# A two-block transformer on one core: the mixer's heads without rotation or mean matmuls, their ends split, inverse roots on GpSimd

## The reference, cut to what matters

```python
p = h @ w_in                                    # split into rq rk rv rg gq gf gi gg ca cb gates
q = _rope(heads(rq, 4), positions)              # [t1*cos - t2*sin, t1*sin + t2*cos], halves of 64
k = _rope(heads(rk, 4), positions) * 128 ** -0.5
o = _retention(q, k, heads(rv, 4))              # o_t = sum_{s<=t} gamma^(t-s) (q_t.k_s) v_s
mu = o.mean(-1, keepdims=True)
o = (o - mu) * lax.rsqrt(jnp.square(o - mu).mean(-1, keepdims=True) + 1e-5)
u_a = o * ret_norm_g * jax.nn.silu(rg)

o = _hgrn2(silu(gq), logf, -expm1(logf), gi)    # gated recurrence, chunkwise
o = o * lax.rsqrt(jnp.square(o).mean(-1, keepdims=True) + 1e-5)
u_b = o * hgrn_norm_g * jax.nn.silu(gg)

u_c = silu(layer_norm(causal_dwconv(ca * sigmoid(cb), 31 taps)))
y  = sigmoid(gates0) * (u_a @ w_branch[0]) + sigmoid(gates1) * (u_b @ w_branch[1])
y += sigmoid(gates2) * (u_c @ w_branch[2])
return y @ w_out
```

## Time and profile before

| what | value |
|---|---|
| median of 3 runs | 3512.76 us (3499.04 to 3517.75) |
| the profiled execution's own time | 3506.1 us |
| its span, first to last instruction | 3504.3 us |
| mean granted TensorE clock | 0.986 of full speed |
| TensorE busy | 3335.8 us, 15280 matmuls |
| VectorE, ScalarE, GpSimd busy | 2126.9, 1306.1, 616.4 us |
| mixer of layer 0, from its first piece | about 1524 to 2110 us of the span |
| mixer of layer 1 | about 2514 to 3090 us of the span |

### The profile page before, as it was taken

How to read it: one execution, slowest core, us unless ns; L and a number is a source line. 1 busy time by engine, 2 the same in 40 slices (tenths; PEclk the granted TensorE clock), 3 DMA queues, 4 the chain that set the end, 5 groups by cost and what they waited for, 6 DMA issues and landing times. The chain is left out here.

```text
span 3504.3 us, 38804 instructions
## 1 busy us (share of the span) xinstructions
PE 3335.8 (95%) x15280; PEld 2662.9 (76%) x15280; DVE 2126.9 (61%) x2701; ACT 1306.1 (37%) x1684; POOL 616.4 (18%) x496
## 2 busy tenths in 40 slices
PE   8899999999999999989999998999898999989997
PEld 6577788886677788877777876888676777768886
DVE  8853566448654766477556746554676557465545
ACT  4664322234663322233332234243433322343323
POOL 2222222121212212201000132010201001320002
PEclk9999999999999999999999999999999999999999
DMA  4122555322123454232112222222221112222221
GB/s 133 37 68 85 186 192 192 108 96 65 39 78 132 181 192 168 91 112 72 61 55 66 91 99 89 96 96 93 75 85 60 61 55 90 96 73 96 97 97 71
DMA packets 72180, 344.43 MB, mean 98 GB/s; under 512 B 25152, under 2 KB 26048, under 8 KB 35648
## 3 DMA queue, kind: packets, MB, share of 16 engines
q1 hardware_dynamic: 70416, 339.12, 28.2%
q0 software_dynamic: 576, 2.33, 0.2%
q10 hardware_dynamic: 1008, 0.51, 0.1%
HBM read 340.51 MB, written 2.10 MB: 98 GB/s over the span
## 5 line engine op out<-in xcount | busy, mean ns | idle before, releaser
L893 PE MATMUL bank<-Hhi_b,whi_b 128*128 128x512 f32 x2976 | 1220.2, 410 | 62.3 <-ACT Hhi_b L2048 22.1
L894 PE MATMUL bank<-Hhi_b,wlo_b 128*128 128x512 f32 x2976 | 1170.5, 393 | 0.0
L900 PE MATMUL bank<-Hlo_b,whi_b 128*128 128x512 f32 x2976 | 1160.9, 394 | 0.8 <-DVE Hlo_b L2329 0.8
L871 DVE TENSOR_TENSOR wlo_b<-raw_b,whi_b 128x2048 fp32r<-128x2048 f32 (+2 forms) x290 | 626.6, 2161 | 487.7 <-ACT whi_b L865 487.5
L893 PEld LDWEIGHTS bank<-Hhi_b,whi_b 128*128 128x128 f32 x2976 | 566.3, 190 | 212.8 <-issue 43.7
L894 PEld LDWEIGHTS bank<-Hhi_b,wlo_b 128*128 128x128 f32 x2976 | 566.6, 190 | 125.4 <-issue 13.8
L900 PEld LDWEIGHTS bank<-Hlo_b,whi_b 128*128 128x128 f32 x2976 | 563.9, 190 | 124.9 <-DVE Hlo_b L2329 4.2
L865 ACT ACTIVATE whi_b<-raw_b 128x2048 fp32r<-128x2048 f32 (+2 forms) x290 | 511.6, 1764 | 368.4 <-PE bank L900 364.4
L893 PE MATMUL bank<-Uhi_b,whi_b 128*128 128x512 f32 x1024 | 405.7, 396 | 11.3 <-POOL Ulo_b L982 11.3
L894 PE MATMUL bank<-Uhi_b,wlo_b 128*128 128x512 f32 x1024 | 399.8, 390 | 0.0
L900 PE MATMUL bank<-Ulo_b,whi_b 128*128 128x512 f32 x1024 | 386.2, 390 | 0.0
(11 more groups left out here) (257 smaller groups left out, 3460.3 us busy)
## 6 DMA issues: line engine op xcount, KB each, us to landing
raw_b<-in_w SPq DMA_DIRECT2D x234, 1024.0 KB, 4.9
ada_b<-in_wada SPq DMA_DIRECT2D x48, 1024.0 KB, 7.0
raw_b<-in_w SPq DMA_DIRECT2D x40, 512.0 KB, 3.8
raw_b<-in_w SPq DMA_DIRECT2D x16, 768.0 KB, 4.3
rel_b<-in_rel SPq DMA_DIRECT2D x128, 24.0 KB, 2.4
X_keep<-in_x SPq DMA_DIRECT2D x4, 512.0 KB, 9.5
decay_b<-in_decay POOLq DMA_DIRECT2D x2, 1024.0 KB, 6.9
out<-X_keep SPq DMA_DIRECT2D x8, 256.0 KB, 2.0
```

What stands on the lines that cost most here:

```text
L871: self.nc.vector.tensor_tensor(self.wlo[n % RAW_SLOTS][:, 0:words], self.raw[n % RAW_SLOTS][:, 0:words], self.whi[n % HI_SLOTS][:, 0:words ...
L893: self.nc.tensor.matmul(out, whi[:, k, cols], xhi, start=(k == 0), stop=False)
L894: self.nc.tensor.matmul(out, wlo[:, k, cols], xhi, start=False, stop=False)
L900: mm = self.nc.tensor.matmul(out, whi[:, k, cols], xlo, start=False, stop=(k == nk - 1))
```

## The change

- `rrot`: the matmul with `rot128` is gone. ScalarE's evacuation of rq and rk writes two tiles: `qf` as before, and `qr` with the halves of the partitions exchanged and one negated (three ScalarE instructions in place of one). GpSimd multiplies `qf` by cos, VectorE `qr` by sin, VectorE adds. This is done right behind the evacuation, not in the chain.
- `omean`: the matmul, the subtraction and its place in the chain are gone. In its stead the transposes of v of a retention head become float32 matmuls with `center` (identity minus 1/128), so that v is already without its mean over the head's width.
- The square is taken by ScalarE from the bank for both kinds of head, ahead of the copy `ON`.
- The root: ScalarE writes mean square plus eps (Identity), and GpSimd raises it to the power -0.5, in a new item `orec`. VectorE's reciprocal and ScalarE's Sqrt are gone for the 16 heads; the convolution's norm and the layer norms keep them.
- `orec` and `oend` are a group of their own; where another head follows in the chain, `orec` is joined to its second group and `oend` to its fourth. `finish` doesn't wait for them. Behind the last head they have an empty group between.
- `taps_beside`: one tap beside each group of a retention head (two before), one beside every other `level` (none before), the free number beside `orec`.
- The gates: branch 0 is done for all eight columns before branch 1 begins.

```diff
-    return heads, mixed(0, 0) + mixed(1, 0) + mixed(0, 1) + mixed(1, 1), mixed(2, 0) + mixed(2, 1)
+    return heads, mixed(0, 0) + mixed(0, 1) + mixed(1, 0) + mixed(1, 1), mixed(2, 0) + mixed(2, 1)
...
-    if not kinds or kinds == ["oend"]:
+    if not kinds or kinds[0] == "orec":
         return free
...
-    if group[0][2] == "r":
-        return 1 if "oss" in kinds else 2
-    return 0
+    if kinds[0] == "level":
+        return group[0][4] % 2
+    return 1 if group[0][2] == "r" else 0
...
-            while any(item[2:4] == (branch, h) for group in chain for item in group):
+            while any(item[2:4] == (branch, h) and item[0] not in ("orec", "oend") for group in chain for item in group):
...
-            if chain and chain[-1][0][0] == "oend":
-                groups = (groups[0] + chain.pop(),) + groups[1:]
+            if chain and chain[-1][0][0] == "orec":
+                orec, oend = chain.pop()
+                groups = groups[:1] + (groups[1] + (orec,), groups[2], groups[3] + (oend,)) + groups[4:]
...
             s.add("evp", l, t, i)
+            if t in ("rq", "rk"):
+                run(("rrot", l, "r", i, t))
...
-                    first = [(item("rrot", "rq"),), (item("rrot", "rk"),), (item("vt2"),)]
-                    first += [(item("rscore", j),) for j in range(TT)] + [(item("rpv"),), (item("omean"),)]
+                    first = [(item("vt2"),)]
+                    first += [(item("rscore", j),) for j in range(TT)] + [(item("rpv"),)]
...
-                follow(*first, (item("oss"),), (item("oend"),))
+                follow(*first, (item("oss"),), (item("orec"), item("oend")))
+                if (b, i) == ("h", 3):
+                    orec, oend = chain.pop()
+                    chain.extend(((orec,), (), (oend,)))
...
+            elif kind == "orec":
+                rs = ("rs", *a)
+                pool.wait_ge(*after("root", *rs))
+                pool.wait_ge(*after("half"))
+                ng.tensor_tensor(buf(rs), buf(rs), keep.half[:, 0:1].to_broadcast([P, SEQ]), ALU.pow).then_inc(*mark("pool", ("recip",) + rs))
...
+                elif t in ("rq", "rk"):
+                    qf_, qr_ = ("qf", l, t, i), ("qr", l, t, i)
+                    half = P // 2
+                    reuse(act, qr_)
+                    act_e.activation(buf(qr_)[0:half], z[half:P], ACT.Copy, scale=-1.0)\
+                        .then_inc(*mark("act", ("qr low", l, t, i)))
+                    act_e.activation(buf(qr_)[half:P], z[0:half], ACT.Copy).then_inc(*mark("act", qr_))
+                    reuse(act, qf_)
+                    act_e.activation(buf(qf_), z, ACT.Copy).then_inc(*mark("act", qf_, ("free", job)))
...
-                k.root(act, None, ("oss", l, b, h), ("rs", l, b, h), 1.0 / P, EPS2)
+                act_e.activation(buf(rs), k.out_of(job)[:], ACT.Identity, bias=keep.eps[EPS2][:, 0:1], scale=1.0 / P)\
+                    .then_inc(*mark("act", ("root",) + rs, ("free", job)))
...
-                k.root(None, dve, ("oss", l, b, h), rs, 1.0 / P, EPS2)
...
                 for t in range(TT):
-                    mm = nt.transpose(k.out_of(job)[:, tile(t)], buf(v)[:, tile(t)], keep.ident[:])
+                    if b == "r":
+                        mm = nt.matmul(k.out_of(job)[:, tile(t)], buf(v)[:, tile(t)], center[:], start=True, stop=True)
+                    else:
+                        mm = nt.transpose(k.out_of(job)[:, tile(t)], buf(v)[:, tile(t)], keep.ident[:])
```

More of the change, by code:

```diff
@@ L573, in run @@
             kind = item[0]
-            if kind in ("rrot", "vt2", "rscore", "omean", "oss", "level", "cross", "cmean", "css"):
+            if kind in ("vt2", "rscore", "oss", "level", "cross", "cmean", "css"):
                 s.small.take(item)
@@ L622, in evacuate @@
                 s.temp("qf", 4, ("qf", l, t, i))
+                s.temp("qr", 2, ("qr", l, t, i))
             if t in ("rv", "gi"):
@@ L1043, in __init__ @@
         self.eps = {EPS1: mem.put("eps1", [P, 1]), EPS2: mem.put("eps2", [P, 1])}
+        self.half = mem.put("half", [P, 1])
         mem.line()
@@ L1700, in block_two @@
     k.bank = banks
-    rot128 = mem.put("rot128", [P, P])
+    center = mem.put("center", [P, P])
     vec = mem.put("vec", [P, DEPTH, NV2])
@@ L1732, in block_two @@
     um = mem.again(ulo_at + 4 * SEQ * 4, ulo_at + 8 * SEQ * 4)
-    t1 = [um.put(f"t1{i}", [P, SEQ]) for i in range(2)]
-    t2 = um.put("t2", [P, SEQ])
+    qr = [um.put(f"qr{i}", [P, SEQ]) for i in range(2)]
+    um.at += SEQ * 4
     pos_i = um.put("pos_i", [P, SEQ], I32)
@@ L1848, in pool_work @@
                 ng.memset(Up[:, :, 0:PAD], 0.0).then_inc(*mark("pool", ("pad", l)))
+                if l == 0:
+                    ng.memset(keep.half[:], -0.5).then_inc(*mark("pool", ("half",)))
             elif kind in ("evout", "evdown") and 1 <= a[-1] <= 3 and (kind == "evout" or a[1] == len(FFN_PARTS) - 1):
@@ L1973, in act_work @@
                 job = (kind, l, b, h)
+                reuse(act, ("on", l, b, h))
                 act.wait_ge(*after(*job))
[L1975 to L1984, removed]
                 reuse(act, ("sq", l, b, h))
-                act_e.activation(buf(("sq", l, b, h)), ON[:], ACT.Square).then_inc(*mark("act", ("sq", l, b, h)))
+                act_e.activation(buf(("sq", l, b, h)), k.out_of(job)[:], ACT.Square)\
+                    .then_inc(*mark("act", ("sq", l, b, h)))
+                act_e.activation(ON[:], k.out_of(job)[:], ACT.Copy).then_inc(*mark("act", ("on", l, b, h), ("free", job)))
             elif kind == "oss":
                 l, b, h = a
-                k.root(act, None, ("oss", l, b, h), ("rs", l, b, h), 1.0 / P, EPS2)
+                job, rs = ("oss", l, b, h), ("rs", l, b, h)
+                reuse(act, rs)
+                act.wait_ge(*after(*job))
+                act_e.activation(buf(rs), k.out_of(job)[:], ACT.Identity, bias=keep.eps[EPS2][:, 0:1], scale=1.0 / P)\
+                    .then_inc(*mark("act", ("root",) + rs, ("free", job)))
             elif kind == "oend":
@@ L2163, in dve_work @@
                 name = ("RQ" if t == "rq" else "RK", l, b, h)
-                u, rot = buf(("t1", l, b, h, t)), ("rrot", l, b, h, t)
+                u, v = buf(("qf", l, t, h)), buf(("qr", l, t, h))
                 if l == 0 and h == 0 and t == "rq":
                     dve.wait_ge(*after("tab2", 1))
[L2167 to L2172, removed]
+                dve.wait_ge(*after("qr", l, t, h))
+                nv.tensor_tensor(v, v, sin[:], ALU.mult).then_inc(*mark("dve", ("q sin", l, t, h)))
+                dve.wait_ge(*after("q cos", l, t, h))
+                dve.wait_ge(*after("q sin", l, t, h))
                 reuse(dve, name)
-                nv.tensor_tensor(buf(name), u, t2[:], ALU.add)\
-                    .then_inc(*mark("dve", name, ("free", ("t1", l, b, h, t)), ("free", ("t2", l, b, h, t)),
-                                    ("free", ("qf", l, t, h))))
+                nv.tensor_tensor(buf(name), u, v, ALU.add)\
+                    .then_inc(*mark("dve", name, ("free", ("qr", l, t, h)), ("free", ("qf", l, t, h))))
             elif kind == "rscore":
@@ L2188, in dve_work @@
                     .then_inc(*mark("dve", ("at", l, b, h, j), ("free", ("rscore", l, b, h, j))))
[L2189 to L2194, removed]
             elif kind == "oss":
                 l, b, h = a
-                rs = ("rs", l, b, h)
-                if b == "h":
-                    dve.wait_ge(*after("on", l, b, h))
+                dve.wait_ge(*after("on", l, b, h))
                 dve.wait_ge(*after("GG", l, b, h))
@@ L2358, in pe_work @@
                 k.products(pe, seen, *a)
[L2359 to L2366, removed]
             elif kind == "vt2":
@@ L2392, in pe_work @@
                 mm.then_inc(*mark("pe", job, ("free", ("at", l, b, h)), ("free", ("VV", l, b, h))))
[L2393 to L2397, removed]
             elif kind == "oss":
@@ L2535, in rotation @@
         return m
+    center = (np.eye(P) - 1.0 / P).astype(np.float32)
     def inv(half):
@@ L2553, in constants @@
     level = np.stack([(s // (2 * L) == s.T // (2 * L)) & (s // L % 2 == 0) & (s.T // L % 2 == 1) for L in LEVELS], 1)
-    return dict(ident=ident, ones=ones, bd64=bd64, rot64=rotation(32), rot128=rotation(64), inv64=inv(32),
+    return dict(ident=ident, ones=ones, bd64=bd64, rot64=rotation(32), center=center, inv64=inv(32),
                 inv128=inv(64), maskA=maskA, maskB=maskB, decay=decay.astype(np.float32),
```

20 lines of the change are left out of this document (9 added, 11 removed).

## The result

| kernel | median | profiled execution |
|---|---|---|
| before | 3512.5 us (4 runs, 3499.0 to 3517.8) | span 3504.3 us, clock 0.986 |
| changed | 4586.1 us (4 runs, 4584.9 to 4588.2) | span 4586.4 us, clock 0.869 |

The ratio is 1.307, 95% interval 1.304 to 1.310. The forecast was 3445 us. First the page of the changed kernel, parts 1 and 2: busy time by engine, and the busy tenths and the clock in 40 slices.

The account below looks back on a forecast made before the run. TensorE, busy 95%, was taken as the bound. 3506.1 - 17.2 (matmuls) - 47.2 (waits) - 20 (clock) + 2.8 + 5.2 (added) + 13.4 (power) = 3443.1, said as 3445 us; range 3418 to 3492.

Parts of the forecast that it names:

- the term for the power: GpSimd's power at the heads: taken as 8 us, bound from above 19, adding 13.4 us over two layers.
- the rival of a long power: Power at the heads: each microsecond past 6, 10 or 12 is paid; 3514 us at 14, 3598 at 20; chance 0.12.
- The slack: Behind the heads, TensorE waits from a power of 6 us (retention 1, 3), 10 (retention 0, 2), about 12 (HGRN).
- TensorE's work: Rotation -13.8 us, mean -6.9, v's two-pass products +3.5: sum -17.2 us, all on the path.
- The waits: TensorE's mixer waits for k, levels, squares and the last HGRN head's low part go in both layers: -47.2 us.
- the sum without the power: The whole kernel's forecast without what GpSimd's power adds: 3429.7 us.
- The clock: Over the heads in both layers, the granted 0.97 goes back to full without the waits: -20 us.
- What is added: Start of layer 0: +2.8 us, wait about 10.5; waits for the last AT: 1.3 us twice a layer, +5.2.
- idle enough: ScalarE gets 32 more instructions of 0.6 us, loses 16 roots' table switches, and was said to have room.
- The rival of mutual hold-up: GpSimd's power and VectorE slow each other at the levels, three heads a layer: +28 us, 3473; chance 0.15.

Follow-up runs that it names:

- pow_quarter: The changed kernel with GpSimd's power on only the first 128 of 512 columns: 3599.8 us, ratio 1.026 to the kernel before.
- mult_for_pow: The changed kernel with GpSimd's power turned into a product with the same tile: 3426.9 us, ratio 0.977 to the kernel before.
- rot_matmul: The changed kernel with old root and reciprocal, rotations one slot later and done by TensorE's float32 matmul again: 3438.2 us, ratio 0.981 to before.
- taps_back: The changed kernel with the old root and reciprocal and the old numbers of taps put back: 3463.8 us, ratio 0.988 to the kernel before.
- ln_exp: The changed kernel with the inverse root on ScalarE alone, as Ln then Exp, nothing on GpSimd: 3442.6 us, ratio 0.982 to the kernel before.
- experiment 5: Two variants of the changed kernel: ScalarE's root with VectorE's reciprocal in orec, 3451.2 us; inverse root by ScalarE's Ln and Exp, 3442.6 us.

## Why the prediction was wrong, step by step

**The step that failed** is the term for the power: "I take 8", with 19 us as the bound from above. It is 82. The mechanism was the one named (VectorE and ScalarE held from the sum of squares until the power ends), and the rival of a long power had the way the time would go: "from about 13.5 us on nothing is gained". The size was off tenfold, and the bound fourfold: the ratio of VectorE's reciprocal to its plain product, 4.9, was taken for what a power costs on another engine. No row bore on that, so the range should have been open above, and the chance of a long power larger than 0.12. With 82 us in it, the rival's own rule gives 3430 + 2·(2·76 + 2·72 + 3·70 + 7·1.7) = 4466 us, 120 below the 4586; the eighth head in the table below, 136.5 us in both layers, is more than that, and the rest of its errors nearly cancel. The estimate that was worked out from the Trainium skill (GPSIMD Engine Reference, § 3.1), 4.3 to 8.5 us, fell with it: what it rested on was my count of 30 to 60 operations. By that rule, as an estimate, 0.159 us a column at 1.2 GHz would be about 190 cycles and some 570 operations. No run here shows whether the rule holds for a power.

**The slack** (how long a power may be before TensorE waits) was read less well than the total of pow_quarter suggests. In the changed kernel it is 82 less the wait:

| behind | predicted slack | wait | slack found |
|---|---|---|---|
| retention heads 1 and 3 | 6 | 73.6, 76.7 | 8, 5 |
| retention heads 0 and 2 | 10 | 66.3, 66.5 | 16 |
| HGRN heads 0 to 2 | 12 | 64.8 to 65.0 | 17 |
| HGRN head 3 | no wait | 68.2 | 14 |

The last line was wrong: branch 1's projection was moved away, but ScalarE's split for `oend` also stands ahead of the gates' sigmoids (L950), which hold the banks of branch 0. So it is eight heads a layer. Behind retention head 1 the wait stood at another place than forecast: not for a panel's low part but at L2373, for ScalarE's copy of the next head's v. Behind head 3 it stood where forecast, at the first level.

At 20.7 us (pow_quarter) the hand count gave 3598 and the chip 3599.8. That closeness is partly luck, as the waits one by one show. These are four rows of TensorE's waits in pow_quarter, whole kernel, and under them the forecast at 20.7 us (us for each head):

```profile
PE bank L2410 <- DVE RQ_b L2229: 31.0, 2, 15.5
PE bank L2373 <- ACT vf_b L1980: 24.9, 2, 12.4
...
PE bank L2410 <- DVE RK_b L2247: 21.6, 6, 3.8
...
PE bank L897 <- ACT sg_b L950: 14.1, 2, 7.0
```

| behind | forecast | pow_quarter, with the wait for the next panel |
|---|---|---|
| retention head 3 | 14.7 | 15.5 |
| retention head 1 | 14.7 | 12.4 + 3.4 |
| retention heads 0 and 2 | 10.7 | 5.0 + 3.8, 5.3 + 4.4 |
| HGRN heads 0 to 2 | 8.7 | 3.5 to 3.8 |
| HGRN head 3 | no wait | 7.0 |

In both layers the waits come to 135 us, where the count (done at 20 us) had 144. TensorE's busy time is 37.3 us above mult_for_pow's (3333.3 against 3296.0), where the count had 24 for the clock. The HGRN heads' slack was too small by some 5 us each, the last head was missed and a drop of the clock costs more than 1.7 us; these errors nearly cancel. The forecast's own term at 8 us is also at odds with that rule: (2 + 3) and one drop of the clock for two waits, where the rule gives 2 + 2 and two drops. And its lower end, 3418, is 2.5 us below what its terms add up to (3429.7 - 5.2 - 4 = 3420.5).

**TensorE's work**, -17.2 us: the rows of rotation and mean are gone, and v's passes doubled. TensorE's busy time in mult_for_pow is 3296.0 against 3335.8, 39.8 us less, which holds the clock as well (forecast for both, 37.2). But rot_matmul shows that in this order the 13.8 us of the rotation are worth 2.5; "all on the path" was not right for it.

**The waits**, -47.2 us: right in what goes. In mult_for_pow the waits of the earlier trace rows for k, for the levels and for the squares are gone, and the 3.5 us at the last head are gone from its row (1.9 left). The reason given was incomplete: without the spread of the taps 14 us of waits come back at the last `AT` and the squares (taps_back). So that the sum without the power lies 3 us from mult_for_pow doesn't prove its terms one by one.

**The clock**, -20 us: right for the heads, a little less over all. mult_for_pow's stretch of the heads is granted 1.00, where it was 0.97. By the mean clocks, (1 - 0.986)·3504 = 49 us of work were lost before and (1 - 0.990)·3423 = 34 are lost now, 15 less:

```profile
1575.00:1905.00 330.00, 326.58 (x1588) 268.65 (x1587) 212.88 (x315) 102.32 (x129) 29.55 (x22) 1.00 0.21 72
```

**What is added**: the wait at the start is 9.8 us, forecast 10.5, before 7.7; the waits for the last `AT` are 1.33 us, four times, 5.3 in all, forecast 1.3 and 5.2. That ScalarE is "idle enough" holds for mult_for_pow, in which no wait names its new evacuations; ln_exp, with more for it to do, is 16 us slower (experiment 5).

**The rival of mutual hold-up** falls but for the power's first microsecond, and there it goes both ways. At three of the 16 heads an operation of VectorE begins with the power or up to 0.08 us behind it, and VectorE is stretched: a tap takes 1.59 us in place of 0.75 (shown in the first timeline), the sum that ends a rotation 1.51 in place of 0.69. At three others a tap began 0.06 us ahead of the power: it keeps its 0.75, and the power takes 82.5 us in place of 81.9. Later in a power nothing is stretched; 3 us into the power of HGRN head 0 the scaling of head 1's q takes 0.69. The changed kernel's timeline at these three places:

```profile
1697.53 81.93 POOL L1892 TENSOR_TENSOR rs_b<-rs_b,half_keep 128x512 f32<-128x512 f32 x1
1697.61 1.51 DVE L2189 TENSOR_TENSOR RQ_b<-qf_b,qr_b 128x512 f32<-128x512 f32 x1 [1.31 <-POOL qf_b L1887]
...
1817.06 0.75 DVE L2155 SCALAR_TENSOR_TENSOR acc_b<-Up_b,vec_b,acc_b 128x512 f32<-128x512 f32 x1
1817.12 82.47 POOL L1892 TENSOR_TENSOR rs_b<-rs_b,half_keep 128x512 f32<-128x512 f32 x1 [7.95 <-ACT rs_b L2005]
...
2047.16 81.92 POOL L1892 TENSOR_TENSOR rs_b<-rs_b,half_keep 128x512 f32<-128x512 f32 x1 [43.68 <-ACT rs_b L2005]
...
2050.15 0.69 DVE L2229 TENSOR_TENSOR RQ_b<-RQ_b,FT_b 128x512 f32<-128x512 f32 x1
```

So it costs under 1 us a head, not the 3 us and a drop of the clock at which the rival was priced.

The Trainium skill's rule on the shared interface (GPSIMD Engine Reference, § 8) is not contradicted: the start agrees with it, and behind the start a power at 0.16 us a column has little to read. That it reads its operands ahead at the start is my guess.

## What to carry to other kernels

An operation that no row shows on its engine has no bound from above; a ratio seen on one engine need not hold on another, so measure it alone first, or give the long end the chance that you can't argue away. Work given to the idlest engine is free only while the engines that read it don't stand in order behind it: look for who is held, since the waits name them and not the slow one. And where the same chain feeds TensorE from several engines, take one matmul away and its time may come back as a wait for the engine that now does that work. Last, a total that comes out right is not yet a proof of its terms: set them beside the waits one by one, as pow_quarter shows.

## What the runs showed of the hardware

- GpSimd's float32 power: 81.92 us for 512 columns, 20.72 us for 128, the same on 64 and on 128 partitions and for the exponents -0.5 and 1.0. That is 24 times VectorE's reciprocal of the same tile and some 60 times GpSimd's product.
- Beside a running power VectorE's two-input operations keep their time (0.69 us). One that begins with the power or up to 0.08 us behind it takes 1.51 to 1.59 us (0.69 and 0.75 else); where a tap began 0.06 us ahead it kept its time and the power took 0.55 us longer.
- After a wait of 65 to 77 us TensorE, granted half its clock while idle, is busy 3.1 us longer for the same work (49.3 us over 16 heads); after waits of 4 to 16 us it is 2.3 (37.3 over 16).
- ScalarE's switch of tables takes 1283 ns in the heads, every time. Ln and Exp, one behind the other, need one each here.
- A ScalarE evacuation of 64 partitions takes 0.59 us, as one of 128 does (0.60).
